# Six ring slots and a longer split lead in the second block, and two more modulation rows computed on VectorE

## The chip, the cores and the metric

One NeuronCore of a Trainium2 chip runs the whole program. The metric is the device time of one execution in microseconds (us). Engines are named as in the profile: PE (TensorE), PEld (its weight loads), DVE (VectorE), ACT (ScalarE), POOL (GpSimd), SP (SyncE, which here only issues DMAs).

## What is computed

Two transformer blocks on 256 tokens of width 1024, all in float32, batch 1. The parts that matter here:

```
# first block: 3 attention branches, then gated merge and output projection
proj = rms_norm(x) @ w_in
merged = sum over a,b,c of sigmoid(gm_br) * ((y_br * silu(g_br)) @ w_up_br)
x = rms_norm(x + merged @ w_o)
# second block, two layers (layer 0: neighbourhood attention + HGRN2; layer 1: short conv)
mod   = silu(c) @ ada_w[layer] + ada_b[layer]      # 6 vectors of 1024 per layer
mod_c = silu(c_ctx) @ ada_w[0] + ada_b[0]
y = mixer(modulate(rms_norm(x), shift_m, scale_m)) @ w_out ; x = x + gate_m * y
h = modulate(rms_norm(x), shift_f, scale_f)
a, val = split(h @ w_up) ; x = x + gate_f * ((gelu(conv3(a)) * val) @ w_down)
```

## The kernel before

**Units.** Every weight is read once. `plan_units` lists the loads in order: a unit is a load of up to 1 MB into one of the four slots of `raw`. The issuing engine SP takes the units strictly in order. It waits with unit u until unit u-4 is released. Most units are weight tiles of 1024 x 256. Such a unit has two halves of 128 x 1024; units of kind U or V (`up_*`, `evoA`, `evoB`) are half as large and have one.

**Splitting.** A matmul in full float32 is made of three products of reduced words. So each half is split: ACT casts it to `whi` (L1097), DVE subtracts, `wlo = raw - whi` (L1634), and PE multiplies (L514 to L516: 24 products of 256 columns per half). `whi` and `wlo` are rings of `WRING = 4` halves. ACT may overwrite a ring place when PE has used the half four before it. DVE's subtraction releases the slot of `raw`. In the code, `ahead(u)` on ACT and on DVE splits the unit after u: a lead of one unit. All engines run programs written out in order, so whatever stands behind `ahead` on ACT or DVE waits with it.

**Modulation rows.** The twelve vectors of `mod` (rows 0 to 11, row n is `ada_w` columns of layer n // 6) take four units of 1 MB each. For most rows PE multiplies straight from `raw` (L615, kind "A", sixteen matmuls of 32 columns wide weights per unit as the trace counts them), ACT copies the result to `arow` (L1120), POOL folds it (L2273, L2274), PE sums it (`sum_ada`, L639) and DVE adds the bias (`keep_ada`, L1675). Such a unit is released by PE. For the rows in `ON_VECTOR` (kind "G") DVE multiplies and accumulates (`add_rows`, L1692 and L1694, two instructions per unit) and releases the unit; PE then spreads the row once over partitions (`spread`, L624), ACT copies that (`keep_spread`, L1129), and the sum is as before. The table `ADA_PLACES` says where in the program each unit of a row stands.

**Stages** (by the profile's time): up to 197 us the slots (`slot0` to `slot13`: first projections and attention, with modulation units in between), 197 to 314 us the gates (twelve pairs `gm_*`, `up_*`), then `wo`, the second block's projections, `na0` to `na9` (neighbourhood attention, with `evoB0` to `evoB3`), `evoA0` to `evoA3` (592 to 609 us; each followed on DVE by an addition to `xT`, L2021, and on ACT by squares, L1524), the first feed forward (`fa0.i` and `fv0.i`, i = 0 to 10, to 743 us; `fd0.i`, to 807 us), the layer-1 mixer (`od*`, `odo`) and the second feed forward.

**A step of the up projections** (`feed_forward`): PE does `fa` and `fv`, each into one of the two banks of `psG`. ACT copies `fa` out (L1561) and does the centre tap (L1544); DVE does `ahead(fa)`, the side taps (L2155, L2157), `ahead(fv)`, then multiplies by `fv` from its bank (L2180), which frees the bank, and splits the product (L1644, L1645). ACT's Gelu stands between side taps and product.

**The end of `evoA`.** PE sums squares in `psY` for the norm: `sum_part` g = 1 takes what POOL folded (L648), g = 2 and 3 wait for ACT's squares (L652). ACT turns the sum to `rn` (L1161, L1162), DVE and ACT make the next inputs `Hhi`, `Hlo` (`normed`, L1707, L1716) tile by tile.

Of the kernel before, what the change touches and what calls it, by code (L numbers as in the profile page):

```python
# [22 lines left out]
P = 128  # L23
D = 1024
# [10 lines left out]
WRING = 4  # L35
HALF = 1024
# [25 lines left out]
ON_VECTOR = (2, 8, 11)  # L62
ADA_ORDER = (0, 1, 2, 3, 10, 4, 5, 6, 7, 8, 9, 11)
ADA_PLACES = {0: ("slot0", "slot1", "slot2", "slot3"), 1: ("slot4", "slot5", "slot6", "slot7"),
# [8 lines left out]
def plan_units():  # L73
# [76 lines left out]
def build(nc, x, norm_gain, w_in, b_forget, lambda_q1, lambda_k1, lambda_q2, lambda_k2, subln_gain, sinks,  # L150
# [26 lines left out]
    with ExitStack() as ctx:  # L177
# [98 lines left out]
        with ExitStack() as a3:  # L276
# [5 lines left out]
            s6("under_rows", [P, 4, D])  # L282
# [89 lines left out]
        def ada_row(n):  # L372
            return arow0[:, n % 2, :] if n < 4 or n == 10 else arow1[:, n - 4 if n < 10 else 0, :]
# [50 lines left out]
        IN_DOWN = (8, 11)  # L424
        UP_SUMS = ({1: 5, 3: 6, 5: 7}, {})
# [83 lines left out]
        def _(pe):  # L509
# [281 lines left out]
            for i in range(4):  # L791
                for b, br in enumerate("abc"):
# [6 lines left out]
                    ada(f"gates{i}{br}")  # L799
# [5 lines left out]
                    elif (i, br) == (1, "b"):  # L805
                        sum_ada(3)
                    elif (i, br) == (3, "b"):
                        pe.wait_ge(turned_kept, 8)
                        sum_ada(10)
                if i == 1:  # L810
                    pe.wait_ge(ada_kept, 4)
# [178 lines left out]
            for n, u in enumerate(SPAN["evoA"]):  # L990
                project(u, Hhi, Hlo)
                if n == 0:
                    pe.wait_ge(pT_kept, NT0 + 2 * NA)
                    sum_ada(4)
                else:
                    sum_part(F["ffn0"], n - 1)
            sum_part(F["ffn0"], 3)
            tail_ada(0)

            def feed_forward(layer):  # L1000
                following = F[("mix1", "last")[layer]]
                for i in range(FT // 2):
# [3 lines left out]
                    if i in UP_SUMS[layer]:  # L1006
                        sum_ada(UP_SUMS[layer][i])
                for i in range(FT // 2):
# [4 lines left out]
                    if i < FT // 2 - 1:  # L1013
# [9 lines left out]
                        if i == 7:  # L1023
                            spread(IN_DOWN[layer])
                        elif i == 9:
                            sum_ada(IN_DOWN[layer])
# [49 lines left out]
        def _(act):  # L1076
# [9 lines left out]
            def split_through(u):  # L1086

                while half_at[0] < H0[u] + NH[u]:
# [5 lines left out]
                    if h >= WRING:  # L1094
# [1271 lines left out]
```

## Time and profile before

| | us |
|---|---|
| median of three runs (1124.33 to 1125.63) | 1125.09 |
| the profiled execution | 1119.25 |
| its span | 1117.5 |
| PE busy | 1065.8 |
| DVE busy | 761.4 |
| ACT busy | 582.0 |

The profiled execution is 1.75 us longer than its span (what lies around the first and the last instruction) and 5.84 us below the median of the three runs. PE is busy for 95% of the span at a mean granted clock of 0.992. An idle time in brackets belongs to the engine of that row, with what ended it.

### The profile page before, as it was taken

The page shows a single profiled execution, that of the slowest core. Times are in us where ns is not written, and L with a number is a line of the kernel's source. Part 1 is how long each engine was busy: PE and PEld are TensorE (multiplying, and loading weights), DVE is VectorE, ACT ScalarE, POOL GpSimd, SP SyncE. Part 2 cuts the span into 40 slices and gives each one's busy share as a digit, 9 for nine tenths or more (in the row PEclk, how much of TensorE's full clock was granted, in tenths as well). Part 3 has the DMA queues.
Part 4 walks back from the last instruction along what each step waited for, and adds up shares of the span by engine and source line. Part 5 has one row for each costly group of instructions (what it writes and reads, how often), then busy time and mean ns, then how long its engine had stood idle before and what let it go on. Part 6 is the DMA issues. An engine that isn't in the chain of part 4 may idle for free.

```text
span 1117.5 us, 21719 instructions
## 1 busy us (share of the span) xinstructions
PE 1065.8 (95%) x9182; PEld 1005.6 (90%) x9182; DVE 761.4 (68%) x1119; ACT 582.0 (52%) x879; POOL 76.2 (7%) x87
## 2 busy tenths in 40 slices
PE   6999999999999999999997999999999989999997
PEld 5988888899999999988576999999989989999997
DVE  6467777654677685985775867777475767767763
ACT  5555655544455674733654656453454446565433
POOL 2000000100102450000101000000010010000000
PEclk9999999999999999999999999999999989999999
DMA  8556666796754675342965755557565535555561
GB/s 270 173 186 234 221 179 217 245 279 207 232 188 149 173 191 188 120 146 77 329 237 192 235 193 174 189 186 300 192 227 189 176 127 189 185 192 169 220 254 38
DMA packets 165773, 219.79 MB, mean 197 GB/s; under 512 B 4481, under 2 KB 146205, under 8 KB 165676
## 3 DMA queue, kind: packets, MB, share of 16 engines
q1 hardware_dynamic: 164442, 215.67, 58.6%
q0 software_dynamic: 832, 1.65, 0.8%
q8 instruction: 73, 1.20, 0.4%
q10 hardware_dynamic: 402, 1.08, 0.4%
q14 instruction: 24, 0.20, 0.1%
HBM read 217.27 MB, written 1.11 MB: 195 GB/s over the span
## 4 chain that ended last, share of the span: by engine, by line
PE 49%; DVE 5%; ACT 2%; issue 1%; POOL 0%; DVEq 0%; ACTq 0%
PE psG L514 11%; PE psG L516 11%; PE psG L515 11%; PE psS L514 4%; PE psS L516 4%; PE psS L515 4%; PE psY L652 1%; DVE stat L2113 1%; DVE wlo L1634 1%; PE psG L615 1%; ACT whi L1097 1%; DVE xT L2021 1%; DVE Hlo L1716 0%; DVE psS L2111 0%; DVE vt L1707 0%
## 5 line engine op out<-in xcount | busy, mean ns | idle before, releaser
L1634 DVE TENSOR_TENSOR wlo<-raw,whi 128x1024 fp32r<-128x1024 f32 x311 | 374.6, 1243 | 126.9 <-ACT whi L1097 121.4
L514 PE MATMUL psG<-Hlo,whi 128*128 128x256 f32 x1520 | 436.0, 287 | 14.2 <-DVE Hlo L1716 4.6
L515 PE MATMUL psG<-Hhi,wlo 128*128 128x256 f32 x1520 | 429.4, 283 | 0.0
L516 PE MATMUL psG<-Hhi,whi 128*128 128x256 f32 x1520 | 429.4, 283 | 0.0
L1097 ACT CAST whi<-raw 128x1024 fp32r<-128x1024 f32 x311 | 315.2, 1048 | 128.3 <-DMA raw<-in_ffn_w_down_dram 37.8
L514 PEld LDWEIGHTS psG<-Hlo,whi 128*128 128x128 f32 x1520 | 288.2, 190 | 21.0 <-issue 11.5
L515 PEld LDWEIGHTS psG<-Hhi,wlo 128*128 128x128 f32 x1520 | 288.3, 190 | 0.1
L516 PEld LDWEIGHTS psG<-Hhi,whi 128*128 128x128 f32 x1520 | 288.1, 190 | 0.0
L514 PE MATMUL psS<-Glo,whi 128*128 128x256 f32 x352 | 99.9, 284 | 0.0
L516 PE MATMUL psS<-Ghi,whi 128*128 128x256 f32 x352 | 99.1, 281 | 0.0
L515 PE MATMUL psS<-Ghi,wlo 128*128 128x256 f32 x352 | 99.1, 281 | 0.0
L514 PEld LDWEIGHTS psS<-Glo,whi 128*128 128x128 f32 x352 | 66.3, 188 | 0.9 <-issue 0.8
L515 PEld LDWEIGHTS psS<-Ghi,wlo 128*128 128x128 f32 x352 | 66.3, 188 | 0.1
L516 PEld LDWEIGHTS psS<-Ghi,whi 128*128 128x128 f32 x352 | 66.3, 188 | 0.0
L2155 DVE SCALAR_TENSOR_TENSOR fz<-fa,pcol,fz 128x255 f32<-128x255 f32 x52 | 25.1, 483 | 59.7 <-ACT fz L1544 58.8
L1561 ACT COPY fa<-psG 128x512 f32<-128x512 f32 x22 | 12.9, 586 | 94.7 <-PE psG L516 94.7
L514 PE MATMUL psG<-Xlo,whi 128*128 128x256 f32 x192 | 55.3, 288 | 1.1 <-DVE wlo L1634 1.1
L515 PE MATMUL psG<-Xhi,wlo 128*128 128x256 f32 x192 | 54.0, 281 | 0.0
L516 PE MATMUL psG<-Xhi,whi 128*128 128x256 f32 x192 | 54.0, 281 | 0.0
L514 PE MATMUL psG<-wlo,Hhi 128*128 128x256 f32 (+1 forms) x144 | 41.1, 286 | 2.8 <-DVE wlo L1634 2.8
L1544 ACT ACTIVATE fz<-fa,pcol 128x256 f32<-128x256 f32 x52 | 31.3, 602 | 17.7 <-DVEq L2218 16.1
L515 PE MATMUL psG<-whi,Hlo 128*128 128x256 f32 (+1 forms) x144 | 40.4, 281 | 0.0
(383 smaller groups left out, 1626.4 us busy)
## 6 DMA issues: line engine op xcount, KB each, us to landing
raw<-in_ada_w_dram SPq DMA_DIRECT2D x48, 1024.0 KB, 6.1
raw<-in_ffn_w_up_dram SPq DMA_DIRECT2D x44, 1024.0 KB, 5.0
raw<-in_w_in_dram SPq DMA_DIRECT2D x29, 1024.0 KB, 7.7
raw<-in_ev_w_in_dram SPq DMA_DIRECT2D x26, 1024.0 KB, 5.4
raw<-in_ffn_w_down_dram SPq DMA_DIRECT2D x22, 1024.0 KB, 5.4
raw<-in_od_w_in_dram SPq DMA_DIRECT2D x12, 1024.0 KB, 5.2
raw<-in_w_in_dram SPq DMA_DIRECT2D x9, 512.0 KB, 5.7
raw<-in_w_o_dram SPq DMA_DIRECT2D x4, 1024.0 KB, 5.2
```

What stands on the lines that cost most here:

```text
L514: mm(o, a_hi, b_lo, start=first, stop=False, skip_group_check=shared)
L515: mm(o, a_lo, b_hi, start=False, stop=False, skip_group_check=shared)
L516: return mm(o, a_hi, b_hi, start=False, stop=last, skip_group_check=shared)
L615: last = mm(bank(u)[32 * j:32 * j + 32, 0:256], cs[:, UNITS[u][2] + k, :], w[:, k, j * 256:(j + 1) * 256], start=(k == 0), stop=(k == 1))
L652: last = mm(psY[:, 0:S], ones[:, 0:P], sqv[:, k, :], start=False, stop=(k == KT - 1))
L1097: nc.scalar.copy(ring_half(whi, v, i), src).then_inc(hi_split, 1)
L1544: ins = nc.scalar.activation(z[:, q, :], src[:, q, :], ACT.Identity, scale=pcol[:, w + q:w + q + 1], bias=pcol[:, b + q:b + q + 1])
L1561: nc.scalar.copy(fa[:, i % 2, :, :], src).then_inc(bank_free[B0[ua] % 2], 1)
L1634: V.tensor_tensor(ring_half(wlo, v, h - H0[v]), src, ring_half(whi, v, h - H0[v]).bitcast(F32), ALU.subtract).then_inc(lo_split, 1)
L2021: ins = V.scalar_tensor_tensor(xT[:, k, :], bank(u)[:, q * S:(q + 1) * S], mod[:, layer, 8 * s + k, 0:1], xT[:, k, :], ALU.mult, ALU.add)
L2113: then(V.tensor_reduce(stat[:, st, 0:2], psS[:, 2 * (s % 2):2 * (s % 2) + 2, :], AX.X, ALU.max, negate=True), biased, NG + s + 1)
L2155: step(V.scalar_tensor_tensor(z[:, q, 1:S], src[:, q, 0:S - 1], pcol[:, w[0] + q:w[0] + q + 1], z[:, q, 1:S], ALU.mult, ALU.add))
```

## The change

Two parts.

1. **Ring.** From `evoB0` on (`DEEP`, the number of its first half) the rings have six places: two more, `whi2` and `wlo2`, lie where only a placeholder was. ACT's wait changes from the half four before to the half six before (`taken`). From `evoA0` on, `ahead(u)` splits two units ahead instead of one (`reach`).
2. **Rows.** Rows 5 and 10 move to `ON_VECTOR`: eight units that PE multiplied are now multiplied by DVE, in steps 1 to 5 and 7 to 9 of the first up projections. The order of rows changes too: row 3 leaves `slot12`, `slot13`, `gates0a`, `gates0b` for `na0` and `na1`; row 10 leaves the gates; rows 4, 6, 7 share the rest of `na`, so `na` has sixteen units on PE as before, and the gates and the last two slots have none. The sum of row 3 moves to the end of `evoA0`, that of row 4 to the end of `evoA1`, those of 6, 7 and 5 to steps 1, 2 and 6, that of row 10 to `fd0.2`. The squares of `ffn0` are summed after all four `evoA` units instead of between them.

```
-ON_VECTOR = (2, 8, 11)
-ADA_ORDER = (0, 1, 2, 3, 10, 4, 5, 6, 7, 8, 9, 11)
+ON_VECTOR = (2, 5, 10, 8, 11)
+ADA_ORDER = (0, 1, 2, 3, 4, 6, 7, 5, 10, 8, 9, 11)
...
-              2: ("slot8", "slot9", "slot10", "slot11"), 3: ("slot12", "slot13", "gates0a", "gates0b"),
-              10: ("gates1a", "gates1b", "gates2a", "gates2b"), 4: ("na0a", "na0b", "na1a", "na1b"),
-              5: ("na2a", "na2b", "na3a", "na3b"), 6: ("na4a", "na4b", "na5a", "na6a"),
-              7: ("na7a", "na8a", "na9a", "na9b"), 8: ("fd0.0", "fd0.2", "fd0.4", "fd0.5"),
+              2: ("slot8", "slot9", "slot10", "slot11"), 3: ("na0a", "na0b", "na1a", "na1b"),
+              4: ("na2a", "na2b", "na3a", "na3b"), 6: ("na4a", "na4b", "na5a", "na6a"),
+              7: ("na7a", "na8a", "na9a", "na9b"), 5: ("up0.1", "up0.2", "up0.3", "up0.4"),
+              10: ("up0.5", "up0.7", "up0.8", "up0.9"), 8: ("fd0.0", "fd0.2", "fd0.4", "fd0.5"),
...
-            s6("under_rows", [P, 4, D])
+            whi2, wlo2 = s6("whi2", [P, MORE, HALF], F32R), s6("wlo2", [P, MORE, HALF], F32R)
...
+        DEEP = H0[SPAN["evoB"][0]]
         def half(ring, h):
-            return ring[:, h % WRING, :]
+            n = (h - DEEP) % (WRING + MORE)
+            if h < DEEP:
+                return ring[:, h % WRING, :]
+            if n < MORE:
+                return (whi2 if ring is whi else wlo2)[:, n, :]
+            return ring[:, (DEEP + n - MORE) % WRING, :]
+        def taken(h):
+            return h + 1 - WRING if h < DEEP else h + 1 - WRING - MORE
+        def reach(u):
+            w = after[u]
+            if u >= SPAN["evoA"][0] and w in after and H0[after[w]] + NH[after[w]] <= H0[u] + WRING + MORE:
+                return after[w]
+            return w
...
-        IN_DOWN = (8, 11)
-        UP_SUMS = ({1: 5, 3: 6, 5: 7}, {})
+        UP_SUMS, UP_SPREAD = ({1: 6, 2: 7, 6: 5}, {}), ({5: 5, 10: 10}, {})
+        DOWN_SUMS, DOWN_SPREAD = ({2: 10, 9: 8}, {9: 11}), ({7: 8}, {7: 11})
...  PE, evoA
                 if n == 0:
                     pe.wait_ge(pT_kept, NT0 + 2 * NA)
+                    sum_ada(3)
+                elif n == 1:
                     sum_ada(4)
-                else:
-                    sum_part(F["ffn0"], n - 1)
-            sum_part(F["ffn0"], 3)
+            sum_squares(F["ffn0"])
...  ACT
-                    if h >= WRING:
-                        act.wait_ge(half_used, h - WRING + 1)
+                    if taken(h) > 0:
+                        act.wait_ge(half_used, taken(h))
...  ACT and DVE
             def ahead(u):
                 if u in after:
-                    split_through(after[u])
+                    split_through(reach(u))
...  DVE, feed_forward
                     ahead(ua)
+                    add_rows(f"up{layer}.{i}")
                     z, src = fz[:, i % 2, :, :], fa[:, i % 2, :, :]
```

On DVE, around `evoA1` to the norm before the first feed forward (`raw` slots and rings, additions to `xT`, `mod` is `keep_ada`), the order before:

```order
L1634 TENSOR_TENSOR wlo<-raw,whi 128x1024
L2021 SCALAR_TENSOR_TENSOR xT<-psG,mod,xT 128x256 x2
L1634 TENSOR_TENSOR wlo<-raw,whi 128x1024
L2021 SCALAR_TENSOR_TENSOR xT<-psG,mod,xT 128x256 x2
L1675 TENSOR_TENSOR mod<-psX,pcol 128x2x4 x2
L2147 SCALAR_TENSOR_TENSOR cm<-mod,pcol 128x8
L1634 TENSOR_TENSOR wlo<-raw,whi 128x1024
L2021 SCALAR_TENSOR_TENSOR xT<-psG,mod,xT 128x256 x4
L1634 TENSOR_TENSOR wlo<-raw,whi 128x1024 x2
L1707 SCALAR_TENSOR_TENSOR vt<-xT,cm,rn 128x256 x2
```

and with the change:

```order
L1651 TENSOR_TENSOR wlo<-raw,whi 128x1024
L1651 TENSOR_TENSOR wlo2<-raw,whi2 128x1024
L2034 SCALAR_TENSOR_TENSOR xT<-psG,mod,xT 128x256 x2
L1692 TENSOR_TENSOR mod<-psX,pcol 128x2x4 x2
L1651 TENSOR_TENSOR wlo2<-raw,whi2 128x1024
L2034 SCALAR_TENSOR_TENSOR xT<-psG,mod,xT 128x256 x2
L1692 TENSOR_TENSOR mod<-psX,pcol 128x2x4 x2
L2162 SCALAR_TENSOR_TENSOR cm<-mod,pcol 128x8
L1651 TENSOR_TENSOR wlo<-raw,whi 128x1024 x2
L2034 SCALAR_TENSOR_TENSOR xT<-psG,mod,xT 128x256 x4
L1651 TENSOR_TENSOR wlo<-raw,whi 128x1024 x2
L1724 SCALAR_TENSOR_TENSOR vt<-xT,cm,rn 128x256 x2
```

The split of `evoA2` now stands before the first addition, both halves of `fa0.0` before the third, and the pair before the norm is `fv0.0`. On ACT, the same place before (`L1524` are the squares):

```order
L1097 CAST whi<-raw 128x1024 x2
L1524 ACTIVATE tok<-xT 128x512
L1097 CAST whi<-raw 128x1024
L1524 ACTIVATE tok<-xT 128x512
L1097 CAST whi<-raw 128x1024 x2
L1524 ACTIVATE tok<-xT 128x512 x2
L1161 ACTIVATE rn<-psY,eps 128x256
```

and with the change:

```order
L1113 CAST whi<-raw 128x1024
L1113 CAST whi2<-raw 128x1024 x2
L1537 ACTIVATE tok<-xT 128x512
L1113 CAST whi<-raw 128x1024 x2
L1537 ACTIVATE tok<-xT 128x512
L1113 CAST whi<-raw 128x1024 x2
L1537 ACTIVATE tok<-xT 128x512 x2
L1175 ACTIVATE rn<-psY,eps 128x256
```

The second square now stands behind the casts of `fa0.0`, the third behind those of `fv0.0`. On DVE, one step of the first up projections, before:

```order
L1634 TENSOR_TENSOR wlo<-raw,whi 128x1024 x2
L2155 SCALAR_TENSOR_TENSOR fz<-fa,pcol,fz 128x255
L2157 SCALAR_TENSOR_TENSOR fz<-fa,pcol,fz 128x255
L2155 SCALAR_TENSOR_TENSOR fz<-fa,pcol,fz 128x255
L2157 SCALAR_TENSOR_TENSOR fz<-fa,pcol,fz 128x255
L1634 TENSOR_TENSOR wlo<-raw,whi 128x1024 x2
L2180 TENSOR_TENSOR fz<-fz,psG 128x512
L1644 CAST Ghi<-fz 128x512
L1645 TENSOR_TENSOR Glo<-fz,Ghi 128x512
```

and step 2 with the change:

```order
L1651 TENSOR_TENSOR wlo<-raw,whi 128x1024 x2
L1711 SCALAR_TENSOR_TENSOR arow<-raw,cs,arow 128x1024 x2
L2170 SCALAR_TENSOR_TENSOR fz<-fa,pcol,fz 128x255
L2172 SCALAR_TENSOR_TENSOR fz<-fa,pcol,fz 128x255
L2170 SCALAR_TENSOR_TENSOR fz<-fa,pcol,fz 128x255
L2172 SCALAR_TENSOR_TENSOR fz<-fa,pcol,fz 128x255
L1651 TENSOR_TENSOR wlo<-raw,whi 128x1024 x2
L2196 TENSOR_TENSOR fz<-fz,psG 128x512
L1661 CAST Ghi<-fz 128x512
L1662 TENSOR_TENSOR Glo<-fz,Ghi 128x512
```

Two row instructions now stand between the split of the next `fa` and the side taps.

## Rows read from the trace of the kernel before

**Rows 1.** The page's head: span, and busy time of each engine (share, instructions).

```profile
span 1117.5 us, 21719 instructions
PE 1065.8 (95%) x9182; PEld 1005.6 (90%) x9182; DVE 761.4 (68%) x1119; ACT 582.0 (52%) x879; POOL 76.2 (7%) x87
```

**Rows 2.** Waits of PE from 550 us on: who, us in total, times, longest.

```profile
PE psG L514 <- DVE wlo L1634: 2.6, 2, 1.3
```

**Rows 3.** Windows: us, busy PE, PEld, DVE, ACT, POOL, clock, DMA share, GB/s.

```profile
197.20:277.40 80.20, 79.48 (x705) 74.30 (x705) 44.36 (x48) 36.05 (x47) 2.89 (x2) 1.00 0.81 249
626.00:743.00 117.00, 117.00 (x989) 117.00 (x988) 85.39 (x118) 67.15 (x83) 0.00 (x0) 1.00 0.56 185
```

**Rows 4.** PE in order of time, gates: start us, us, instruction, [idle before <- releaser].

```profile
266.06 1.07 PE L615 MATMUL psG<-raw,cs 128*32 128x256 f32 x16
267.06 0.39 PE L514 MATMUL psG<-Hlo,whi 128*128 128x256 f32 x1
...
275.84 1.07 PE L615 MATMUL psG<-raw,cs 128*32 128x256 f32 x16
277.39 0.39 PE L514 MATMUL psG<-Hlo,whi 128*128 128x256 f32 x1 [0.48 <-DVE mt L1889]
```

**Rows 5.** PE in order of time: the first gate projection starts.

```profile
197.14 0.39 PE L514 MATMUL psG<-Hlo,whi 128*128 128x256 f32 x1 [1.44 <-ACT sg L1221]
```

**Rows 6.** ACT in order of time, slots 12 and 13.

```profile
180.43 0.37 ACT L1120 COPY arow<-psG 128x256 f32<-128x256 f32 x1 [1.30 <-PE psG L615]
180.84 2.00 ACT L1097 CAST whi<-raw 128x1024 fp32r<-128x1024 f32 x2
...
193.05 1.05 ACT L1255 CAST Mhi<-sg 128x1024 fp32r<-128x1024 f32 x1 [7.11 <-DVE sg L1779]
```

**Rows 7.** DVE in order of time, slot 13.

```profile
181.99 2.36 DVE L1634 TENSOR_TENSOR wlo<-raw,whi 128x1024 fp32r<-128x1024 f32 x2 [5.11 <-ACT whi L1097]
```

**Rows 8.** PE in order of time: one spread of a row.

```profile
788.94 0.64 PE L624 MATMUL psX<-arow,ones 128*32 128x256 f32 x8
```

**Rows 9.** DVE by line: count, busy us, mean ns, idle before.

```profile
L1694 DVE SCALAR_TENSOR_TENSOR arow<-raw,cs,arow 128x1024 f32<-128x1024 f32 x21 | 26.9, 1282 | 0.5
```

**Rows 10.** DVE in order of time: part of a step of the first up projections.

```profile
675.23 0.68 DVE L2180 TENSOR_TENSOR fz<-fz,psG 128x512 f32<-128x512 f32 x1
...
677.13 2.36 DVE L1634 TENSOR_TENSOR wlo<-raw,whi 128x1024 fp32r<-128x1024 f32 x2
682.27 0.48 DVE L2155 SCALAR_TENSOR_TENSOR fz<-fa,pcol,fz 128x255 f32<-128x255 f32 x1 [2.78 <-ACT fz L1544]
```

**Rows 11.** ACT in order of time, the same step.

```profile
680.38 0.58 ACT L1561 COPY fa<-psG 128x512 f32<-128x512 f32 x1 [4.65 <-PE psG L516]
```

**Rows 12.** DMA issues, 660 to 700 us: count, KB each, us to landing.

```profile
raw<-in_ffn_w_up_dram SPq DMA_DIRECT2D x7, 1024.0 KB, 5.0
```

**Rows 13.** PE in order of time: end of the output projection, starts of two stages.

```profile
603.91 0.70 PE L648 MATMUL psY<-tok,ones 128*128 128x256 f32 x2 [1.98 <-POOL tok L2283]
...
610.79 0.48 PE L652 MATMUL psY<-tok,ones 128*128 128x256 f32 x1 [0.95 <-ACT tok L1524]
...
622.24 0.36 PE L514 MATMUL psG<-Hlo,whi 128*128 128x256 f32 x1 [1.22 <-DVE wlo L1634]
...
821.06 0.36 PE L514 MATMUL psG<-Hlo,whi 128*128 128x256 f32 x1 [1.34 <-DVE wlo L1634]
```

**Rows 14.** Windows as in rows 3, after PE stood idle.

```profile
604.00:608.00 4.00, 4.00 (x21) 3.95 (x22) 0.19 (x1) 2.53 (x3) 0.00 (x0) 0.61 0.80 264
914.00:918.00 4.00, 4.00 (x21) 4.00 (x21) 4.00 (x11) 2.58 (x6) 0.00 (x0) 0.50 0.44 156
```

**Rows 15.** DVE in order of time: splits of `evoA1` and `evoA2`.

```profile
592.60 1.23 DVE L1634 TENSOR_TENSOR wlo<-raw,whi 128x1024 fp32r<-128x1024 f32 x1
...
596.92 1.23 DVE L1634 TENSOR_TENSOR wlo<-raw,whi 128x1024 fp32r<-128x1024 f32 x1
```

**Rows 16.** ACT in order of time, last output projection.

```profile
604.69 1.99 ACT L1097 CAST whi<-raw 128x1024 fp32r<-128x1024 f32 x2 [3.87 <-DMA raw<-in_ffn_w_up_dram]
```

**Rows 17.** DMA issues as in rows 12, 595 to 606 us.

```profile
raw<-in_ffn_w_up_dram SPq DMA_DIRECT2D x2, 1024.0 KB, 5.7
```

More of the change, by code:

```diff
@@ L35 @@
 WRING = 4
+MORE = 2
 HALF = 1024
@@ L106, in plan_units @@
             section(f"up_{br}{i}", "U" if br != "b" else "V", f"w_up_{br}", i * 256, 1)
-            ada(f"gates{i}{br}")
     for i in range(4):
@@ L372, in ada_row @@
         def ada_row(n):
-            return arow0[:, n % 2, :] if n < 4 or n == 10 else arow1[:, n - 4 if n < 10 else 0, :]
+            return arow0[:, n % 2, :] if n < 3 else arow1[:, ROW[n], :]
+        ROW = {3: 0, 4: 1, 6: 2, 7: 3, 5: 4, 10: 5, 8: 0, 9: 1, 11: 2}
         def ada_part(u):
@@ L798, in _ @@
                         sum_squares(F["ctx"])
-                    ada(f"gates{i}{br}")
                     if (i, br) == (0, "a"):
@@ L804, in _ @@
                         sum_ada(2)
[L805 to L809, printed above, removed]
                 if i == 1:
-                    pe.wait_ge(ada_kept, 4)
+                    pe.wait_ge(ada_kept, 3)
                     turn_tokens(1)
@@ L1007, in feed_forward @@
                         sum_ada(UP_SUMS[layer][i])
+                    if i in UP_SPREAD[layer]:
+                        spread(UP_SPREAD[layer][i])
                 for i in range(FT // 2):
@@ L1022, in feed_forward @@
                             last.then_inc(half_used, 1)
[L1023 to L1026, printed above, removed]
+                        if i in DOWN_SPREAD[layer]:
+                            spread(DOWN_SPREAD[layer][i])
+                        elif i in DOWN_SUMS[layer]:
+                            sum_ada(DOWN_SUMS[layer][i])
                     else:
@@ L1117, in keep_rows @@
                     act.wait_ge(ada_done, ON_PE.index(u) + 1)
-                    if q == 0 and n in (3, 10):
-                        act.wait_ge(row_summed, 2 if n == 3 else 3)
                     nc.scalar.copy(ada_row(n)[:, q * 256:(q + 1) * 256], bank(u)[:, 0:256]
@@ L1323, in _ @@
                         high_of(2)
-                    keep_rows(f"gates{i}{br}")
                     if (i, br) == (0, "b"):
@@ L1568, in feed_forward @@
                     act.wait_ge(gelu_out, FT // 2 * layer + i + 1)
+                    if i - 1 in UP_SPREAD[layer]:
+                        keep_spread(UP_SPREAD[layer][i - 1])
                 for i in range(FT // 2):
                     ahead(SPAN[f"fd{layer}.{i}"][0])
-                    if i == 8:
-                        keep_spread(IN_DOWN[layer])
+                    if layer == 0 and i == 1:
+                        keep_spread(10)
+                    elif i - 1 in DOWN_SPREAD[layer]:
+                        keep_spread(DOWN_SPREAD[layer][i - 1])
                 nc.scalar.preload_act_table_set(TABLES)
@@ L1639, in ahead @@
                 if u in after:
-                    split_through(after[u])
+                    split_through(reach(u))
             def split_value(v, hi, lo, s, n):
@@ L1880, in _ @@
                         keep_ada(3)
-                    elif (i, br) == (1, "c"):
-                        keep_ada(4)
-                    elif (i, br) == (3, "c"):
-                        keep_ada(5)
                     dve.wait_ge(gate_e, n + 1)
@@ L2144, in _ @@
                 add_gated(u, n, 0, 2)
-                if n == 1:
-                    keep_ada(6)
+                if n == 0:
+                    keep_ada(SUM_IX[3] + 1)
+                elif n == 1:
+                    keep_ada(SUM_IX[4] + 1)
                     step(V.scalar_tensor_tensor(cm[:, 2, :], mod[:, 0, 32:40, 0], 1.0, pcol[:, C_FFN:C_FFN + 8],
@@ L2190, in feed_forward @@
                         gains(3, 1, C_MIX + 8)
+                    elif layer == 0 and i == 3:
+                        keep_ada(SUM_IX[10] + 1)
                     elif i == 9:
-                        keep_ada(SUM_IX[IN_DOWN[layer]] + 1)
+                        keep_ada(SUM_IX[DOWN_SUMS[layer][i]] + 1)
                 u = SPAN[f"fd{layer}.{FT // 2 - 1}"][0]
@@ L2283, in fold_squares @@
                 G.tensor_tensor(sqv[:, 0, :], sqv[:, 0, :], sqv[:, 1, :], ALU.add).then_inc(sq_folded, 1)
-            for n in (0, 1, 3, 10):
+            for n in (0, 1):
                 fold_row(n)
@@ L2330, in _ @@
             pool.sem_inc(nb_set, 1)
-            for n in (4, 5, 6, 7):
+            for n in (3, 4, 6, 7):
                 fold_row(n)
```

## The prediction

> **What bounds the kernel now.** I read the page first: PE is busy for 1065.8 of 1117.5 us [rows 1]. So what counts is what PE does and the 52 us in which it waits. A second view, the waits of PE from 550 us on, shows what a deeper ring can return at most: PE waits for the low halves of the weights (L1634) twice, 2.6 us in all [rows 2]. Third, the windows by stage. In the first up projections PE never stops (117.00 of 117.00 us, 989 matmuls, so 0.118 us each), while DVE is busy for 85.39 us of them and the DMA engines for 0.56; in the gates PE is busy for 79.48 of 80.20 us, and the DMA engines for 0.81 [rows 3]. So the modulation units sit where PE has no spare time, and they would go where DVE has 27% to spare. Last, the engines in order of time at the places of the change.
>
> **Part A: what leaves PE in the first block.** A modulation unit is one group of 16 matmuls. From its start to the next product are 267.06 - 266.06 = 1.00 us; the last of the gates takes 277.39 - 275.84 = 1.55 us, with a wait for a bank [rows 4]. The rows 3 and 10 had six units in the gates: five at about 1.00 and one at 1.55, **-6.5 us**. I count them in full, because the four gate pairs that have no unit today run with one stall only, which I leave as it is. DVE has 44.36 busy us of 80.20 there, ACT 36.05, and the loads thin out from 2.5 MB to 1.5 MB a pair [rows 3].
>
> The two units of `slot12` and `slot13` stand where PE is late anyway: the first gate projection waits 1.44 us for ACT [rows 5]. ACT is late because it waits 7.11 us for DVE (L1779), and DVE's chain begins with a subtraction that waited 5.11 us for ACT's cast [rows 6, 7]. That cast stood behind the copy of `slot12`'s unit: ACT idled 1.30 us for PE, then copied, and cast at 180.84; without the unit it can cast at 180.43 - 1.30 = 179.13 [rows 6]. The chain moves by 1.7 us, and PE with it: **-1.7 us** (bounds: 0 if the cast finds another wait, 2.0 if both units count in full).
>
> The sums by `sum_ada` are twelve before and after: 0. POOL folds two rows less; nothing on PE waits for those folds, so 0.
>
> **Part B: what comes back to PE.** Two spreads, each 0.64 us busy [rows 8], of which the next product overlaps the end: 0.6 each, **+1.2 us**.
>
> On the eight units, row and rule differ. A unit's 16 matmuls have weights 32 columns wide and start every 0.0625 us [rows 4], a full product every 0.118 us [rows 3]. The Trainium skill (TensorEngine Tiling (Array Packing), section Overview) gives up to 4 times the speed when one dimension is 32 or less. By that, a unit would cost 16 x 0.118 / 4 = 0.47 us, and the eight give back some 4 us less than I count: by my estimate, about -8 in place of -12 in all. The trace shows not quite half of that speed-up, and the trace's 1.00 us is what I use.
>
> **Part C: the eight units on DVE.** A unit is two instructions of 1.282 us [rows 9], 2.6 us. A step lasts 96 x 0.118 = 11.4 us. In it DVE idles 2.78 us before the side taps [rows 10]. The two instructions fit there with 0.1 to 0.2 us to spare: they follow `ahead(fa)` directly. If they end late, the product (L2180) is late, and with it the bank. That bank is wanted when PE has done the next `fa`, which ACT's copy marks at 680.38; the product ended at 675.23 + 0.68 = 675.91 [rows 10, 11]. So DVE may run 4.4 us late before PE notices. The sums in steps 1, 2 and 6 add some 0.25 us each to DVE.
>
> The loads: the load of the next-but-one `fa` waits for the release of the row's unit (four units before). The circle is landing 5.0 us [rows 12], ACT's first cast 1.05 us (half of the 2.00 for a pair, and the latency) [rows 16], two subtractions 2.36, two row instructions 2.6: 11.0 us, against a step of 11.4. It closes, just. Three loads a step are 3.1 MB in 11.4 us, 276 GB/s; rows 3 have 249 GB/s at a share of 0.81, so full use is some 307 GB/s, or 330 by the other row. Cost of part C: **0** (bounds 0 and +4).
>
> **Part D: the end of `evoA`.** PE waits 1.98 us for POOL's fold, and the 24 products of `evoA3` then run at a granted clock of 0.61 on average, most of them at 1.2 GHz instead of 2.4: 21 in 4.00 us, 0.190 us each instead of 0.118, which makes 1.7 us for the 24 [rows 13, 14]. With the squares summed at the end, both go. What ends last is then the third pair of squares on ACT. Today the last sum starts at 610.79 [rows 13]. With the change `evoA2` is split right behind `evoA1`, at 592.60 + 1.23 = 593.8, not at 596.92 [rows 15]. It releases the slot of `fa0.0`, so that load lands 3.1 us sooner, at 604.69 - 3.1 = 601.6 [rows 16]. ACT: casts of `fa0.0` to 603.7, second squares, then the casts of `fv0.0` (landed near 604.5) to 606.7, third squares to 607.3, fourth to 608. The order hides a price: ACT and DVE now wait for a landing before they do squares and additions, and POOL's fold, which needs the second squares, comes later too. So the last sum starts near 608.3 to 609: **-2.2 us** (bounds 0 and -3.7).
>
> **Part E: the second unit of a stage.** `fv0.0` is split before the norm instead of after it: the wait of 1.22 us at 622.24 goes. So does the wait of 1.34 us at 821.06 for `odu0` [rows 13]. **-2.5 us**. The split lead gives nothing in the second feed forward: there DVE has `fv1.0` ready when PE needs it. Behind `fa0.0` the next lateness is `fa0.1`, whose load waits for the first unit of `tail0`; it has a whole unit of PE's time more than it had.
>
> **Sum.** -6.5 - 1.7 + 1.2 + 0 - 2.2 - 2.5 = -11.7 us. The profiled execution, 1119.25 us, would become 1107.5. It is 5.84 us below the median of the runs; I take the gain to be the same on the median: 1125.09 - 11.7 = **1113.4 us**.
>
> **Rivals.**
> 1. **The gates don't give all back.** Some pairs there wait for landings on ACT, and DVE slows beside POOL. Against it: the DMA load falls by two fifths. If two of the six units come back as waits and the slots give nothing: 1113.4 + 2 + 1.7 = 1117.
> 2. **Landings set the pace in the up projections.** With 5.7 us, as between 595 and 606 us [rows 17], the circle of part C is 11.7, 0.3 us more than a step: over eight steps 2.4, inside the 4.4 us of slack, but the sum of row 5 in step 6 needs ACT's spread copy, which stands behind Gelu, and it could be 1 us late. At 6.5 us lateness grows by 1.1 a step and PE stalls some 3 us. 1114 to 1117. The Trainium skill (DMA: Bandwidth & Descriptors, section Bandwidth) lists 6.15 us for 1 MB; the trace's 5.0 is shorter, at a lower load. By it the circle would be 12.2 us, and the kernel, I estimate, 1115.
> 3. **The clock falls before the first feed forward.** At the end of `odo` PE idles between the projection and the next stage, and the clock is then 0.50 from 914 to 918 [rows 14]. Between `evoA3` and `fa0.0` PE will idle in one stretch, not two. The price is like part D's 1.6 us: 1115.
> 4. **Slower: DVE is overfull.** If steps with a row take 2.3 us more than 11.4, for instance because the large instructions stretch beside the denser loads, eight of them cost 18 us, less the 4.4 of slack: 14, more than the 11.7 gained: 1127. It decides above 2.0 us a step, or at a landing of 7.5 us. Against it: between 660 and 700 us landings take 5.0 us, and nothing runs on POOL from 626 to 743 us [rows 3, 12].
> 5. **The change does nothing**: the units leave PE by the order of instructions, so only if PE was not the limit. 95% speak against it.
>
> **Chances.** Forecast 0.62 (its own range 1111 to 1115.5); rival 1 0.12; rival 2 0.11; rival 3 0.09; rival 4 0.03; rival 5 0.03. The range 1109.5 to 1118.0 takes in rivals 1 to 3 and the bounds of D (-3.7) and of the slots. A measurement tells 0.2%, 2.3 us, from no change; all but rivals 4 and 5 lie below that: faster 0.94, same 0.03, slower 0.03.
>
> **What will show it.** L615 has 448 matmuls instead of 576 and no rows between 170 and 314 us; L624's successor 40 instead of 24. The gates stage is 6 to 7 us shorter. In the up projections DVE is busy for 0.9 and more, and PE still has no wait longer than 0.3 us. The wait for POOL at the end of `evoA` is gone and so is the dip of the clock at 604 us. The second unit after each norm starts without a wait for `wlo`. Wrong I would be if PE waited in the up projections, or if the gates kept their length, or if the end of `evoA` took as long as now.

## The result, and the profile after

The changed kernel takes 1129.66 us (median, 1126.2 to 1131.9), the kernel before 1123.45 us on the same chip (1121.27 to 1125.63): ratio 1.0053, 95% interval 1.0040 to 1.0066. It is slower by 6 us, where 11.7 us less were forecast. The time lies outside the forecast range of 1109.5 to 1118.0 us.

Head of the page and the waits of PE from 550 us on, changed kernel, to compare with [rows 1, 2]:

```profile
span 1127.9 us, 21501 instructions
PE 1063.8 (94%) x9070; PEld 1008.3 (89%) x9070; DVE 776.7 (69%) x1135; ACT 578.5 (51%) x873; POOL 71.3 (6%) x83
```

```profile
PE psY L668 <- POOL tok L2301: 10.9, 2, 5.8
PE psS L534 <- DVE wlo L1651: 6.8, 2, 3.9
```

PE is busy for less time (1063.8, not 1065.8 us), and the span is 10.4 us longer. Two waits for POOL's fold of the squares take 10.9 us; before there was one, of 1.98 us [rows 13]. And PE waits for low halves in the down projections (`psS`), where it never waited before.

Starts of the stages on PE tell where the time went. Each number runs from the start of a stage's first matmul to the start of the next stage's, in one profiled execution of each kernel:

| stage, us | before | changed | lead of one | ring and lead alone |
|---|---|---|---|---|
| start to `evoA0` | 592.6 | 581.6 | 585.3 | 594.5 |
| end of `evoA` | 22.0 | 25.9 | 19.6 | 28.3 |
| first up projections | 128.6 | 129.1 | 130.6 | 127.6 |
| first down projection | 70.1 | 81.4 | 71.2 | 81.6 |
| layer-1 mixer | 100.2 | 98.8 | 100.6 | 98.7 |
| second up projections | 127.8 | 128.3 | 127.4 | 128.4 |
| second down projection | 70.0 | 75.9 | 70.3 | 75.6 |

(The last two columns are experiments, below. The profiled execution of the kernel before is 4.2 us shorter than its median here.) The time to `evoA0` falls by 11.0 us in this pair of executions, and by 8.7 on average over all profiles (below); 8.2 were forecast for what leaves PE there. The end of `evoA` loses 3.8 us, the first down projection 11.35, the second 5.9.

Windows of the changed kernel, as in [rows 3, 14]:

```profile
193.60:264.80 71.20, 70.14 (x587) 69.01 (x588) 42.98 (x45) 34.37 (x40) 0.00 (x0) 1.00 0.62 193
620.00:736.00 116.00, 116.00 (x977) 115.34 (x975) 103.28 (x133) 65.95 (x83) 0.00 (x0) 1.00 0.76 260
588.00:594.00 6.00, 6.00 (x53) 6.00 (x51) 1.38 (x5) 0.00 (x0) 0.00 (x0) 1.00 1.04 349
594.00:600.00 6.00, 0.25 (x3) 0.05 (x1) 4.03 (x6) 5.05 (x6) 2.72 (x2) 0.84 0.09 32
600.00:604.00 4.00, 3.91 (x9) 3.19 (x10) 2.54 (x3) 0.63 (x1) 0.04 (x1) 0.50 0.00 0
1085.00:1093.00 8.00, 4.11 (x22) 3.94 (x21) 5.11 (x5) 3.99 (x4) 0.00 (x0) 0.79 0.46 188
```

In the gates the DMA share fell to 0.62. In the up projections PE never stops, with DVE busy for 103.28 of 116 us: part C is as forecast. But from 588 to 594 us the DMA engines are full, and in the next 6 us PE is busy for 0.25. After such a pause comes a clock of 0.50, so that the ten products of the squares' sum, the first work behind it, take 4.6 us (600.09 to 604.65, the next rows).

**The end of `evoA`.** PE, ACT, POOL and DVE in order of time:

```profile
593.97 0.28 PE L536 MATMUL psG<-Hhi,whi 128*128 128x256 f32 x1
600.09 1.22 PE L668 MATMUL psY<-tok,ones 128*128 128x256 f32 x2 [5.84 <-POOL tok L2301]
601.10 3.62 PE L672 MATMUL psY<-tok,ones 128*128 128x256 f32 x8
604.65 2.02 PE L635 MATMUL psG<-raw,cs 128*32 128x256 f32 x32
```

```profile
594.60 1.99 ACT L1113 CAST whi<-raw 128x1024 fp32r<-128x1024 f32 x2 [8.08 <-DMA raw<-in_ffn_w_up_dram]
596.50 0.62 ACT L1537 ACTIVATE tok<-xT 128x512 f32<-128x512 f32 x1
597.24 1.99 ACT L1113 CAST whi<-raw 128x1024 fp32r<-128x1024 f32 x2
```

```profile
597.20 2.03 POOL L2299 TENSOR_TENSOR tok<-tok 128x512 f32<-128x512 f32 x1 [15.89 <-ACT tok L1537]
599.31 0.72 POOL L2301 TENSOR_TENSOR tok<-tok 128x256 f32<-128x256 f32 x1
```

```profile
595.75 2.36 DVE L1651 TENSOR_TENSOR wlo<-raw,whi 128x1024 fp32r<-128x1024 f32 x2 [5.68 <-ACT whi L1113]
598.03 2.15 DVE L2034 SCALAR_TENSOR_TENSOR xT<-psG,mod,xT 128x256 f32<-128x256 f32 x4
```

ACT stands 8.08 us at the casts of `fa0.0` until that load lands. Behind them is the second square, behind that POOL's fold, and PE waits 5.84 us for it. DVE stands 5.68 us at the split of the same unit, and the additions for `evoA2` and `evoA3` (x4) come only then.

**The down projections.** In the second one, SP's issues, ACT's casts and DVE's splits and row instructions:

```profile
1038.66 0.37 SPq L510 DMA_DIRECT2D raw<-in_ada_w_dram  x1
1052.09 0.88 SPq L510 DMA_DIRECT2D raw<-in_ffn_w_down_dram  x2
1053.01 0.47 SPq L510 DMA_DIRECT2D raw<-in_ada_w_dram  x1
1065.50 0.37 SPq L510 DMA_DIRECT2D raw<-in_ffn_w_down_dram  x1
```

```profile
1056.95 2.00 ACT L1113 CAST whi<-raw 128x1024 fp32r<-128x1024 f32 x2 [10.62 <-DMA raw<-in_ffn_w_down_dram]
...
1070.38 2.00 ACT L1113 CAST whi<-raw 128x1024 fp32r<-128x1024 f32 x2 [8.87 <-DMA raw<-in_ffn_w_down_dram]
```

```profile
1058.11 4.85 DVE L1651 TENSOR_TENSOR wlo<-raw,whi 128x1024 fp32r<-128x1024 f32 x4 [6.05 <-ACT whi L1113]
1062.88 2.60 DVE L1711 SCALAR_TENSOR_TENSOR arow<-raw,cs,arow 128x1024 f32<-128x1024 f32 x2
1071.53 2.36 DVE L1651 TENSOR_TENSOR wlo<-raw,whi 128x1024 fp32r<-128x1024 f32 x2 [6.06 <-ACT whi L1113]
```

The row instructions end at 1062.88 + 2.60 = 1065.48, and at 1065.50 SP issues the next load: it had waited 12 us for that raw slot. The unit in that slot is the load of 1038.66 (the fourth issue before), which took 5.5 us to land: it lay there for some 20 us. Its two instructions stood behind the split of a unit two ahead, which waited (6.05 us). PE pays near the middle of the stage (and the clock is 0.79 on average from 1085 to 1093, last row of the windows):

```profile
1089.19 0.36 PE L534 MATMUL psS<-Glo,whi 128*128 128x256 f32 x1 [3.89 <-DVE wlo L1651]
```

### The profile page after: what moved, and what is told of

Read it like the earlier page. It is cut to its first block, busy times and chain, and to the rows that moved or that the text cites. A ratio compares the mean times of both kernels' runs of the same rounds, so it can differ in the third digit from the quotient of the medians.

```text
span 1127.9 us, 21501 instructions
## 1 busy us (share of the span) xinstructions
PE 1063.8 (94%) x9070; PEld 1008.3 (89%) x9070; DVE 776.7 (69%) x1135; ACT 578.5 (51%) x873; POOL 71.3 (6%) x83
## 4 chain that ended last, share of the span: by engine, by line
PE 39%; DVE 8%; DMA 7%; ACT 3%; issue 1%; POOL 0%; SPq 0%; DVEq 0%; ACTq 0%
PE psG L534 11%; PE psG L536 11%; PE psG L535 11%; DMA raw<-in_ffn_w_down_dram 4%; DVE wlo L1651 3%; DVE arow L1711 1%; ACT whi L1113 1%; DMA raw<-in_ffn_w_up_dram 1%; PE psY L672 1%; PE psS L534 1%; PE psS L536 1%; PE psS L535 1%; DMA raw<-in_od_w_in_dram 1%; DMA raw<-in_ev_w_out_dram 1%; PE psG L635 1%
## 5 line engine op out<-in xcount | busy, mean ns | idle before, releaser
L536 PE MATMUL psS<-Ghi,whi 128*128 128x256 f32 x352 | 100.5, 286 | 0.0
L2170 DVE SCALAR_TENSOR_TENSOR fz<-fa,pcol,fz 128x255 f32<-128x255 f32 x52 | 25.1, 483 | 41.1 <-ACT fz L1557 40.2
L1711 DVE SCALAR_TENSOR_TENSOR arow<-raw,cs,arow 128x1024 f32<-128x1024 f32 x35 | 44.9, 1282 | 0.8
```

Source lines behind the costliest of these rows:

```text
L536: return mm(o, a_hi, b_hi, start=False, stop=last, skip_group_check=shared)
L1711: ins = V.scalar_tensor_tensor(r, w[:, k, :], c, r, ALU.mult, ALU.add)
L2170: step(V.scalar_tensor_tensor(z[:, q, 1:S], src[:, q, 0:S - 1], pcol[:, w[0] + q:w[0] + q + 1], z[:, q, 1:S], ALU.mult, ALU.add))
```

## The experiments

**Theory.** The lead of two units does the harm. `ahead` is an instruction that waits for a landing. With a lead of one it waits for the unit that PE takes next; with a lead of two it waits for the one after that, which is issued later and lands later, and what stands behind it (squares, additions, the row instructions that free a raw slot) waits longer too. ACT's waits for landings in the first down projection are 24.9 us with a lead of one and 39.5 in the changed kernel. **Rivals**: the moved rows (denser loads, more on DVE); the later sum of the squares; the six ring places themselves.

### A lead of one, and a ring of four

```
 def reach(u):
-    if u >= SPAN["evoA"][0] and w in after and ...:
+    if False:
```

> The changed kernel, with the split lead set back to one unit; ring of six, moved rows and the late sum of the squares stay. Theory T1 (the lead of two units does the harm, because splits that wait for a landing stand ahead of the additions to xT, the squares and the row instructions): the stalls at the end of evoA (6.1 us in one gap), at the end of the first down projection (5.4 us) and inside both down projections (11.35 and 5.9 us against before in all) go, and the time is near 1112 us, 0.990 of the kernel before. Rival R1 (the moved rows cost this, by the denser loads and by DVE's extra work): the down projections stay long and the time stays above 1124 us. Rival R2 (the later sum of the squares costs it): the stalls inside the down projections go, the 6 us at evoA stay, about 1118 us.

Measured: 1113.22 us (1110.77 to 1116.39), ratio 0.9921 (0.9902 to 0.9940). Stages in the table above. One condition turns a loss of 6 us into a gain of 9; the moved rows and the late sum are in this kernel too and are not to blame. Then also the ring of four:

```
-    return h + 1 - WRING if h < DEEP else h + 1 - WRING - MORE
+    return h + 1 - WRING
```

(and `half` takes place `h % WRING` throughout.)

> As the run with a lead of one, and the ring has four places again: what is left of the change are the moved rows and the later sum of the squares. T1: with a lead of one unit nobody uses the two more places, so within 1.5 us of that run, near 1112 us. Rival R3 (the six places themselves cost or gain something, by where they lie or by freeing ACT's casts earlier): over 3 us away from the run with a ring of six and a lead of one.

Measured: 1114.33 us, ratio 0.9931 (0.9914 to 0.9948). It overlaps with the lead of one: the places alone do nothing that can be told. The kernel with a lead of one was run a second time, beside the last three kernels of this document and on the same chip as they:

> The kernel with a lead of one again, as the base for the other three of this call on the same chip: ratio 0.990 to 0.994 of the kernel before.

Measured: 1114.13 us, ratio 0.9914 (0.9887 to 0.9941), as expected.

### Ring and lead alone, without the rows

The kernel before, with `half`, `taken` and `reach` of the changed one and nothing else.

> The kernel before with the ring of six and the lead of two alone; no row is moved and the squares are summed where they were. T1: slower than before by what the stages from evoA on lost, 3.8 + 11.35 + 5.9 less 1.4 of the layer-1 mixer, about +14 to +20 us (ratio 1.012 to 1.018). R1 (rows) and R2 (sum of the squares): same as before or up to 2.5 us faster, since the waits of 1.22 and 1.34 us for the second unit after a norm go.

Measured: 1143.65 us (1142.70 to 1145.51), ratio 1.0195 (1.0176 to 1.0215): 21 us slower than before, just above the 14 to 20 that were expected, and in the same three stages (last column of the table). So the lead costs 21 us where no row is moved, and 15 beside the moved rows (1.0053 less 0.9921); what gains is the rows and the late sum, some 9 us. The changed kernel is 15 less 9. Why the lead costs 6 us more in the kernel without the rows isn't shown: the three stages lose alike (6.3, 11.5 and 5.6 us here against the kernel before, 6.3, 10.3 and 5.6 in the changed kernel against the lead of one). In the up projections this kernel takes 127.6 us, 1.0 less than before: the wait of 1.22 us at the second unit [rows 13] is gone.

### A lead of two only in some stages

```
-    if u >= SPAN["evoA"][0] and w in after and ...:
+    if UNITS[u][1][:6] in ("ffn_up", "od_w_i") and w in after and ...:
```

> The changed kernel with the lead of two units only from the up projections and the layer-1 input projections (sources ffn_w_up and od_w_in); one unit from evoA, odo and the down projections. T1: the stalls are gone as with a lead of one, and the lead of two is harmless in the up projections, where PE had no wait with it: within 1 us of the run with a lead of one everywhere, about 1112 us. If the lead of two in the up projections were what makes the later loads late (the loads of the first down units), it stays above 1116 us.

Measured: 1115.79 us, ratio 0.9940 (0.9922 to 0.9958). Both down projections are as long as with a lead of one (71.1 and 70.3 us). The median is 2.6 us above the lead of one, where 1 us at most was expected; the intervals (0.9902 to 0.9940 there) don't tell the two apart. The first up projections take 130.5 us, as with a lead of one, and the wait at the second unit is there (1.24 us): what the lead gives in that stage is this unit, split before the norm, and it takes a lead of two in `evoA`. The other way round, only in the down projections (`"ffn_do"`):

> The changed kernel, but the lead is two units only in the two down projections. T1: only these have the circle of landing, split and release in less time than it takes, so both down stages are as long as in the changed kernel (81.4 and 75.9 us, against 71.2 and 70.3 with a lead of one), the evoA stage is as with a lead of one (19.6 us), 1127 to 1129 us. If the harm in the down stages were inherited from loads that are late since evoA or the up projections, both would be near 71 and the time near 1114 us.

Measured: 1133.76 us, ratio 1.0110 (1.0091 to 1.0129). The down projections take 83.5 and 78.6 us, `evoA` 19.6: the harm in the down stages is their own and isn't inherited. It was 5 us and more above what was expected; why these two stages are longer still than in the changed kernel stays open. The stalls for low halves are the longer ones: 4.95 us in the first (2.90 in the changed kernel), 1.32 and 4.23 in the second (3.89).

### Which instruction stands behind the split

Rows first, in the down projections on DVE, lead of two kept:

```
+                    add_rows(f"fd{layer}.{i}")
                     if i < FT // 2 - 1:
                         ahead(SPAN[f"fd{layer}.{i}"][0])
-                    add_rows(f"fd{layer}.{i}")
```

> The changed kernel (ring of six, lead of two), with DVE's two row instructions of a down step ahead of the split instead of behind it, so that the raw slot of the row's unit is released before DVE waits for the landing two units on. T1 in its first mechanism (the slot's release, and through it the load four units later, waits behind a split that itself waits for a landing): the stalls inside the down projections go (gap of 2.9 to 3.9 us near the middle), the second down stage goes from 75.9 back to 70 to 71 us, the first from 81.4 to about 76, and the 6 us at evoA and the 5 us at the end of the first down projection stay: 1118 us, 11 us less than the changed kernel. If the raw slots are not the limit (if the DMA engines are simply full there), both down stages stay and the time is 1128 to 1130 us.

Measured: 1116.34 us (1115.89 to 1117.38), ratio 0.9959 (0.9943 to 0.9975), 0.0094 below the changed kernel's ratio, or 10.6 us. The down projections take 70.9 and 70.3 us (expected about 76, and 70 to 71). The same issues of SP as above, with rows first:

```profile
1042.87 0.88 SPq L510 DMA_DIRECT2D raw<-in_ffn_w_down_dram  x2
1045.27 0.37 SPq L510 DMA_DIRECT2D raw<-in_ada_w_dram  x1
1053.71 0.37 SPq L510 DMA_DIRECT2D raw<-in_ffn_w_down_dram  x1
```

```profile
1048.81 2.36 DVE L1651 TENSOR_TENSOR wlo<-raw,whi 128x1024 fp32r<-128x1024 f32 x2 [3.57 <-ACT whi L1113]
1051.08 2.60 DVE L1711 SCALAR_TENSOR_TENSOR arow<-raw,cs,arow 128x1024 f32<-128x1024 f32 x2
1053.72 2.36 DVE L1651 TENSOR_TENSOR wlo<-raw,whi 128x1024 fp32r<-128x1024 f32 x2
```

SP issues at 1053.71, when the row instructions end (1053.68); the pause between issues is 8.4 us, not 12.5, and PE has no stall. Only the order of two lines on one engine is changed, so the first mechanism is shown. The stall of 5.08 us at the end of the first down projection, which I had put down to squares behind casts, went too: it was the late loads.

Squares first, on ACT, in `evoA` and after the first down projection:

```
 for n, u in enumerate(SPAN["evoA"]):
-    ahead(u)
     if n:
         square_part("ffn0", n - 1)
+    ahead(u)
...
 for g in range(4):
     square_part(("mix1", "last")[layer], g)
+ahead(SPAN[f"fd{layer}.{FT // 2 - 1}"][0])
```

(that split is left out of the loop before it.)

> The changed kernel with ACT's squares ahead of the casts: in evoA the squares of the step before precede the casts of the next split, and after the first down projection the four squares precede the last split. T1 in its second mechanism (squares stand behind casts that wait for a landing, so POOL folds late and PE waits and loses its clock): the gap of 5.8 us at evoA and that of 5.1 us at the end of the first down projection go, the stalls inside the down projections stay: about 1119.5 us. If PE waits there for the landing itself, the gaps stay as waits for wlo and the time stays above 1127 us.

Measured: 1129.07 us, ratio 1.0074 (1.0053 to 1.0095). A miss: the time doesn't fall. `evoA` takes 24.6 us, 1.3 less than in the changed kernel, and the first down projection 80.7, 0.7 less. Both edits together:

> Both reorderings together, lead of two kept. T1: all stalls of the lead go, and the lead keeps what it gave (no waits of 1.2 and 1.4 us for the second unit after a norm): 1110.5 to 1113 us, at least as fast as a lead of one with 1113.2. If a third thing behind the longer lead costs time, 1115 us or more.

Measured: 1116.66 us, ratio 0.9959 (0.9943 to 0.9975), the same as rows first alone. `evoA` still takes 25.1 us. DVE's and ACT's rows of this kernel say why:

```profile
600.77 2.36 DVE L1653 TENSOR_TENSOR wlo<-raw,whi 128x1024 fp32r<-128x1024 f32 x2 [4.01 <-ACT whi L1113]
603.05 2.15 DVE L2036 SCALAR_TENSOR_TENSOR xT<-psG,mod,xT 128x256 f32<-128x256 f32 x4
```

```profile
599.62 1.99 ACT L1113 CAST whi<-raw 128x1024 fp32r<-128x1024 f32 x2 [3.08 <-DMA raw<-in_ffn_w_up_dram]
604.14 0.63 ACT L1537 ACTIVATE tok<-xT 128x512 f32<-128x512 f32 x1 [2.52 <-DVEq L2042]
```

The square now waits for DVE's addition, and that still stands behind DVE's split. So the additions first as well:

```
 for n, u in enumerate(SPAN["evoA"]):          # DVE
-    if n < 3:
+    if n == 0:
         ahead(u)
     add_gated(u, n, 0, 2)
+    if n == 1:
+        ahead(u)
...
+ahead(SPAN["evoA"][2])
 ahead(SPAN["evoA"][3])
```

(on ACT the last `ahead` of `evoA` goes behind the fourth square.)

> The kernel with both reorderings, and at the end of evoA now DVE's additions to xT too stand ahead of its splits (from evoA1 on), and the third and fourth squares ahead of the casts of fv0.0. Theory T1, mended: with squares first on ACT the stage stayed long (25.1 us) because DVE's third addition still stands behind its split of fa0.0, which waits for that landing near 597 us. Expected: the 4.0 us gap goes, the stage takes 20 to 22.5 us (19.6 with a lead of one, plus up to 2 for the split of fv0.0 that now stands ahead of the norm), 1112.5 to 1114.5 us by the scale of the first call. Rival R4 (the landing itself is late because four loads go out at once, and with it the norm): the stage stays above 24 us.

Measured: 1114.40 us (1110.94 to 1116.38), ratio 0.9925 (0.9901 to 0.9949). `evoA` takes 21.6 us, in an execution in which `evoA0` ran at a clock of 0.61; the repetition of the lead of one, with a low clock there too, has 21.1. The gap of 4.0 us is gone. With every split behind the work that others wait for, a lead of two is as good as a lead of one (0.9921 and 0.9914), and no better. Four subtractions instead of two now stand between the last addition and the norm,

```profile
601.35 4.63 DVE L1655 TENSOR_TENSOR wlo<-raw,whi 128x1024 fp32r<-128x1024 f32 x4
605.89 0.87 DVE L1728 SCALAR_TENSOR_TENSOR vt<-xT,cm,rn 128x256 f32<-128x256 f32 x2
```

and PE waits longer for the norm's output than with a lead of one. The waits from 550 us on, of this kernel and then of the lead of one:

```profile
PE psG L534 <- DVE Hlo L1737: 7.4, 3, 2.7
```

```profile
PE psG L534 <- DVE Hlo L1733: 4.6, 3, 2.8
PE psG L534 <- DVE wlo L1651: 3.7, 3, 1.4
```

2.8 us more for `Hlo` (1.8 before `fa0.0`, 1.0 before the mixer) stand against the 3.7 us of waits for `wlo` that the lead takes away: 1.06 at `evoA3`, and 1.22 and 1.38 at the second units of the up projections and the mixer. And the longer pause before `fa0.0` brought the clock down. The first 3 us of the up projections, of this kernel and of the changed one:

```profile
607.64:610.64 3.00, 3.00 (x14) 3.00 (x15) 3.00 (x9) 1.86 (x4) 0.00 (x0) 0.51 1.06 357
```

```profile
607.51:610.51 3.00, 3.00 (x24) 2.97 (x24) 3.00 (x9) 1.86 (x4) 0.00 (x0) 1.00 1.04 350
```

The stage takes 130.0 us instead of 129.1: 2.8 + 0.9 = 3.7, so the losses eat up the gain.

### The late sum, and the piece of the lead that is worth keeping

Lead of one, and the squares of `ffn0` summed between the `evoA` units again:

```
-            sum_squares(F["ffn0"])
+                if n:
+                    sum_part(F["ffn0"], n - 1)
+            sum_part(F["ffn0"], 3)
```

> Lead of one, and the squares of ffn0 are summed between the evoA units as in the kernel before. Part D's half that concerns the sum: PE waits again about 2 us for POOL's fold and runs evoA3 at half clock, the evoA stage is 22 instead of 19.6 us, and the time is 1.5 to 2.5 us above the lead of one in this call. R2 (the late sum costs time): it is faster than the lead of one.

Measured: 1114.86 us, ratio 0.9929 (0.9910 to 0.9948), against 0.9914 (0.9887 to 0.9941) for the lead of one run beside it: not told apart by the time. By the stage it is: 22.06 us against 21.07, and the wait for POOL is back (1.55 us at 597.26). Both executions had the lower clock at `evoA0`, and in this state the late sum gives 1.0 us. The other half of what was expected didn't come: `evoA3` ran at a clock of 1.00 behind that wait (24 products in 2.93 us), not at half. The kernel before has that fall of the clock [rows 14], and its `evoA0` ran at 1.00; its stage is 2.4 us longer than that of the first lead of one (22.0 and 19.6), but the rows differ there too. So 1.0 us is the late sum without the clock; with it the price is only argued.

Lead of two at the last two units of the first down projection alone, and rows first (the edit shown above, so this kernel has two changes beside the lead of one):

```
-    if u >= SPAN["evoA"][0] and w in after and ...:
+    if u in (SPAN["fd0.9"][0], SPAN["fd0.10"][0]):
```

> Lead of one everywhere, except two units at the last two units of the first down projection, so that odu0 is split before the norm; row instructions ahead of the split in the down projections. T1: only the useful piece of the lead is left, 1.4 us off the layer-1 mixer stage (98.8 instead of 100.5 us), all else as with a lead of one: about 1111.5 us, 1 to 2 us below the lead of one in this call. If the casts of odu0 ahead of the squares cost as much as they give: no difference.

Measured: 1111.80 us (1111.55 to 1112.83), ratio 0.9907 (0.9892 to 0.9922). The mixer stage takes 98.9 us instead of 100.5. It has the lowest median of all, 10.8 us below the kernel before in the same group of runs and about 2 us below the lead of one, though the intervals of these two overlap.

## Why the prediction was wrong, point by point

**Part A** (-8.2) held. Twelve profiles with the rows moved reach `evoA0` at 584.9 us on average (581.6 to 587.8); the two without at 592.6 and 594.5: -8.7. The gates took 117.2 us and take 109.6, 7.5 less (forecast 6.5). Some 0.7 of it isn't the units: the sums of rows 3 and 10 left the gates as well and come back elsewhere; such a sum takes 0.36 us of PE. In the last two slots, from the products with `vc` at 178.44 (176.61) to the first gate projection at 197.14 (193.63), it is 18.7 against 17.0 us, the 1.7 of the forecast. On the Trainium skill's factor of up to 4 (TensorEngine Tiling (Array Packing), Overview), by which the eight units would give back some 4 us less: six units gave 6.8 us, so the row's price stood. But the row doesn't test the factor. The kernel issues eight matmuls of plain float32 per unit, which the trace counts as sixteen, and the full product beside them has reduced words; no run compares the two widths with the same words.

**Part B and C** (+1.2 and 0) held within a microsecond. The up projections take 1.45 us more with a lead of two (129.07 against 127.62 without the rows) and 1.9 with a lead of one; the two spreads are 1.14 of it, and 0.3 to 0.8 stays unplaced. PE had no wait. Landings took 6.0 us in the changed kernel between 660 and 700 us, not 5.0, near the 6.15 of the Trainium skill (DMA: Bandwidth & Descriptors, Bandwidth), and still nothing was late. (That figure of the page is for transfers issued from GpSimd; here SP issues them.) Rival 2 had the size and not the effect. DVE's product and ACT's copy of the next `fa` show how much room there was in a step with a row, in the changed kernel:

```profile
666.95 0.68 DVE L2196 TENSOR_TENSOR fz<-fz,psG 128x512 f32<-128x512 f32 x1
```

```profile
672.02 0.59 ACT L1574 COPY fa<-psG 128x512 f32<-128x512 f32 x1 [2.35 <-PE psG L536]
```

The bank was free at 667.63, 4.4 us before it was wanted, as in the kernel before [rows 10, 11].

**Part E** (-2.5) held: -1.0 in the up projections without the rows, -1.4 in the mixer.

**Part D failed.** The step: "It releases the slot of `fa0.0`, so that load lands 3.1 us sooner". The release and the issue did come sooner: 584.01 is 2.4 us after the start of `evoA0`, before it was 598.17, 5.6 us after it.

```profile
579.09 4.15 SPq L510 DMA_DIRECT2D raw<-in_ada_w_dram  x2
584.01 3.83 SPq L515 DMA_DIRECT2D raw<-in_ffn_w_up_dram  x2
```

But the load landed 13.0 us after that start (594.60) and before at 12.1 (604.69, [rows 16]): it took 10.6 us in place of 6.5. Four loads of 1 MB, two for rows and two for `fa0.0` and `fv0.0`, were issued between 579.09 and 587.8, where the kernel before spread the same four over 13.6 us, and the DMA engines were full (349 GB/s at a share of 1.04, window 588 to 594). From this landing hung two chains. I had seen the one on ACT ("ACT and DVE now wait for a landing before they do squares and additions") and priced it with the wrong landing; the one on DVE, through the third addition, I hadn't followed. Squares first alone and both reorderings alone left this stage at 24.6 and 25.1 us; only with the additions first as well did it fall to 21.6, so both chains are shown. Forecast -2.2; measured +3.8, and +6.3 beside the same kernel with a lead of one. The clock added to it: 9 matmuls in the 4 us after the pause, at 0.50. The ten products of the sum start 0.46 us apart there, with a lead of one and a clock of 1.00 0.22 us apart:

```profile
599.03 0.59 PE L668 MATMUL psY<-tok,ones 128*128 128x256 f32 x2
599.46 1.03 PE L672 MATMUL psY<-tok,ones 128*128 128x256 f32 x4
```

By these rows I estimate the clock's part at 2.4 us.

**The down projections were left out.** I wrote the circle of landing, split and release for the up projections, where it closed, and of the second feed forward only that "The split lead gives nothing"; for the first down projection I wrote no term at all. The same circle is tighter there. In the changed kernel the raw slot of a row's unit was held until the unit two ahead had landed, was cast (2.0), split (2.36) and the row done (2.6). One turn, from the issue at 1052.09 to that at 1065.50, takes 13.4 us and brings two units of `fd1`; PE uses up two of the eleven in 2/11 of 70.0 us, 12.7. With rows first the turn is 1053.71 - 1042.87 = 10.8 us, and the stalls are gone. Price: 10.3 and 5.6 us against the lead of one. These 16 us are the change of sign: with rows first alone the kernel is faster than before (0.9959). The medians show less of them than the stages of single executions do, 10.6 us.

**The rivals.** The slower case I named (DVE overfull in the up projections) had the wrong place. Rival 3 had the place of the clock's fall right and priced it at 1.6 us; the pause itself was the larger part. The forecast without the lead, -11.7 + 2.2 + 2.5, is -7.0 us, and -8.0 with the 1.0 us for the late sum that was measured afterwards; the ring of four with a lead of one gives -0.69%, -7.7 us. So the part on the rows was right and not by luck, and the part on the lead was wrong.

## What to carry to other kernels

On an engine that runs in program order, a prefetch of the next operand is a wait for a landing, and a longer lead is a longer wait for everything behind it: first list what stands behind it (a release of a buffer above all), then put that ahead of it, and only then lengthen the lead. A load that is issued sooner lands sooner only if the DMA engines have room at that moment. Where a change has two parts, cost each in every stage that it touches, also in those where it is meant to do nothing.

## What was not expected of the hardware

After the same pause the clock stays or falls. The first projection of `evoA` starts after 2.0 us without work in all fourteen profiles here, and what PE did before it is the same in all: busy for 2.9 to 3.0 of 3 us with 40 to 42 matmuls, then for 1.0 us with 16 more, all at a clock of 1.00. In seven profiles the 24 products behind the pause start within 2.8 us, in the other seven within 4.0 to 4.4. With a lead of one, in the first run and in its repetition, the 6 us after the pause:

```profile
585.29:591.29 6.00, 6.00 (x50) 6.00 (x51) 3.64 (x6) 1.57 (x2) 0.00 (x0) 1.00 0.89 328
```

```profile
585.48:591.48 6.00, 6.00 (x38) 6.00 (x39) 2.42 (x5) 0.31 (x1) 0.00 (x0) 0.72 0.87 327
```

50 matmuls in the one, 38 in the other, 0.120 and 0.158 us each, at a granted clock of 1.00 and 0.72. The stage is 19.6 or 21.1 us by it, with the same program. Two kernels that differ by as much in one stage must be compared at the same clock. The changed kernel and the first run of the lead of one both had 1.00 there, so their difference of 6.3 us at `evoA` is free of it.
